# A last projection with 21 Strassen slabs in place of 17, and two of their block sums made by GpSimd's transfers

## The reference

```python
x = _layer_norm(DEEPNORM_ALPHA * x + mix, ln1_gain[l], ln1_bias[l])
h = jnp.square(jax.nn.relu(x @ w_ff1[l])) @ w_ff2[l]
x = _layer_norm(DEEPNORM_ALPHA * x + h, ln2_gain[l], ln2_bias[l])
```

## Time and profile before

| | us |
|---|---|
| median of 3 runs | 1241.91 (1241.68 to 1242.8) |
| the profiled execution | 1241.83 |
| its span, first to last instruction | 1240.0 |
| TensorE's granted clock | 0.999 of full speed |

### The profile page before, as it was taken

The page is one execution under the profiler, slowest core; times in us unless marked ns, Lnnn a source line. Parts: engine busy times, 40 slices in busy tenths (PEclk is TensorE's granted clock), DMA queues, the critical chain, the costliest instruction groups (busy, mean ns, idle before and its releaser), DMA issues.

```text
span 1240.0 us, 22985 instructions
## 1 busy us (share of the span) xinstructions
PE 1218.8 (98%) x9585; PEld 1031.9 (83%) x9585; DVE 861.9 (70%) x909; ACT 619.6 (50%) x674; POOL 137.5 (11%) x94
## 2 busy tenths in 40 slices
PE   8999999999999999999999999999999999999996
PEld 8888888888779778888888888888888888888884
DVE  5688887465766375765455555545689998899987
ACT  6754555545666254453434343343455555566651
POOL 0022112000000000055000000000122221022220
PEclk9999999999999999999999999999999999999999
DMA  9454465332421156635555555555565555555541
GB/s 339 150 210 170 172 252 189 104 138 104 170 103 54 54 215 234 242 110 196 192 180 201 174 200 177 195 186 186 199 245 203 202 203 204 188 208 200 200 155 68
DMA packets 34206, 222.38 MB, mean 179 GB/s; under 512 B 4717, under 2 KB 5101, under 8 KB 8782
## 3 DMA queue, kind: packets, MB, share of 16 engines
q1 hardware_dynamic: 34126, 221.21, 50.2%
HBM read 219.10 MB, written 2.10 MB: 178 GB/s over the span
## 4 chain that ended last, share of the span: by engine, by line
PE 55%; DVE 1%; ACT 0%; issue 0%; ACTq 0%; DVEq 0%
PE ps L531 55%; DVE stats L2139 0%; DVE xres L2136 0%; DVE wlo_end L2301 0%; DVE xres L2329 0%; DVE xres L2327 0%; ACT whi_end L1283 0%; DVE xres L2317 0%; ACT xres L1283 0%; DVE xres L2321 0%; ACT shi L1283 0%; DVE moments L2142 0%; PE ps L1175 0%; DVE moments L2149 0%; ACT moments L1283 0%
## 5 line engine op out<-in xcount | busy, mean ns | idle before, releaser
L1712 DVE TENSOR_TENSOR wlo<-stage,whi 128x2048 fp32r<-128x2048 f32 x166 | 387.2, 2333 | 245.7 <-ACT whi L1283 244.9
L531 PE MATMUL ps<-acts,whi 128*128 128x512 f32 (+1 forms) x1728 | 535.0, 392 | 3.4 <-DVE wlo L1739 2.1
L1283 ACT ACTIVATE whi<-stage 128x2048 fp32r<-128x2048 f32 (+2 forms) x196 | 361.9, 1848 | 308.7 <-PE ps L531 303.9
L531 PEld LDWEIGHTS ps<-acts,wlo 128*128 128x128 f32 x1680 | 315.8, 188 | 72.5
L531 PE MATMUL ps<-acts,wlo 128*128 128x256 f32 x1680 | 334.8, 278 | 0.0
L531 PEld LDWEIGHTS ps<-acts,whi 128*128 128x128 f32 x1728 | 264.0, 189 | 8.0 <-DVE wlo L1739 2.3
L531 PE MATMUL ps<-whi,shi 128*128 128x512 f32 x402 | 110.9, 389 | 0.6 <-issue 0.6
L531 PE MATMUL ps<-whi,slo 128*128 128x512 f32 x402 | 110.8, 389 | 0.0
L531 PE MATMUL ps<-wlo,shi 128*128 128x512 f32 x402 | 110.8, 389 | 0.0
L1283 ACT ACTIVATE shi<-hid 128x512 fp32r<-128x512 f32 x64 | 40.5, 632 | 124.1 <-PE ps L531 124.1
L531 PEld LDWEIGHTS ps<-whi,shi 128*128 128x128 f32 x402 | 75.3, 188 | 16.5 <-issue 1.0
(11 more groups left out here) (290 smaller groups left out, 1394.6 us busy)
## 6 DMA issues: line engine op xcount, KB each, us to landing
stage<-w_ff SPq DMA_DIRECT2D x128, 1024.0 KB, 4.8
stage<-w_in SPq DMA_DIRECT2D x48, 1024.0 KB, 4.9
stage<-w_out SPq DMA_DIRECT2D x16, 1024.0 KB, 4.9
stage<-w_in SPq DMA_DIRECT2D x6, 512.0 KB, 9.4
xstage<-xT SPq DMA_DIRECT2D x4, 512.0 KB, 7.4
TM_TT<-eyes SPq DMA_DIRECT2D x4, 512.0 KB, 7.7
xres<-x SPq DMA_DIRECT2D x1, 2048.0 KB, 9.6
gain<-ln_gain SPq DMA_DIRECT2D x2, 1024.0 KB, 7.3
```

The lines of the kernel that those rows point to most:

```text
L531: return pe.matmul(out, lhsT, rhs, start=start, stop=stop, skip_group_check=True)
L1283: return act.activation(out, in_, func, **kw)
L1712: TTn(wlo[k0 % NHL][:, :], stage[k0 % NST][:, :], f(whi[k0 % NHL][:, :]), ALU.subtract).then_inc(s_lo, 1)
```

## The change

The sets of Strassen slabs become 4, 6, 9, 11, ..., 26, 28 and 37, 39, ..., 57, 59: two of every five slabs. `tsum` gets a second buffer (in slot 9, part of the activations of the first projection; `bias2` lies there at the end). The two sums of L2250 go: POOL issues a transfer that copies two weight blocks from memory into `tsum`, and, when it has landed, one that adds a third block to both. Both wait for the landing of the one before. DVE waits for them on `s_lsum` and makes the other two sums. The order of ACT and DVE is changed where the last but one slab was a Strassen slab, for slabs 1 to 3 (pair before weights), and in the last turn (`whi_end`, `wlo_end` before the pair, the third part of `shared_taken` behind it). The loads of `gain2` and `bias2` move behind all slabs. Two semaphores of the start are merged.

```diff
--- before.py
+++ after.py
@@ -51,7 +51,7 @@
 G_END = G_FF2 + DFF // P
 NST, NHL = 4, 2
 
-QUADS = (tuple(range(4, 29, 3)), tuple(range(38, 60, 3)))
+QUADS = ((4, 6, 9, 11, 14, 16, 19, 21, 24, 26, 28), (37, 39, 42, 44, 47, 49, 52, 54, 57, 59))
 QUAD = QUADS[0] + QUADS[1]
 
 
@@ -213,7 +213,7 @@
         bias1 = at("bias1", 13, [P, D])
         shift_diag = at("shift_diag", 12, [P, P])
         shift_row = at("shift_row", 13, [P, 512])
-        tsum = at("tsum", 12, [P, 4, 512])
+        tsums = [at("tsum0", 12, [P, 4, 512]), at("tsum1", 9, [P, 4, 512])]
         thi, tlo = at("thi", 10, [P, 4, 512], F32R), at("tlo", 11, [P, 4, 512], F32R)
         asum = at("asum", 13, [P, 4, P], byte=2048)
         ashi = at("ashi", 13, [P, 4, P], F32R, byte=4096)
@@ -252,12 +252,12 @@
         s_x = [sem(f"x_loaded{i}") for i in range(4)]
         s_xhi, s_xlo = sem("head_piece_rounded"), sem("head_piece_remainder")
         s_cst, s_pos, s_attc, s_levc, s_gup = (
-            sem("consts_loaded"), sem("positions_loaded"), sem("attention_consts_loaded"),
+            sem("constants_and_lora_weights_loaded"), sem("positions_loaded"), sem("attention_consts_loaded"),
             sem("level_masks_loaded"), sem("gate_up_loaded"))
         s_ln1c, s_ln2c, s_xres, s_out = (
             sem("ln1_vectors_loaded"), sem("ln2_vectors_loaded"), sem("x_reloaded"), sem("output_stored"))
         s_vecl, s_lncol = sem("vectors_loaded"), sem("ln1_columns_loaded")
-        s_vec, s_lup = sem("zeros_then_vectors_ready"), sem("lora_weights_loaded")
+        s_vec, s_lsum = sem("zeros_then_vectors_ready"), sem("block_sums_loaded")
         s_lora, s_z, s_sig = sem("lora_activated"), sem("decay_logits"), sem("decay_sigmoid")
         s_item, s_itemd, s_gam = sem("rate_or_cumsum"), sem("rate_or_cumsum_done"), sem("chunk_decay_kept")
         s_ang, s_sin = sem("rotary_table_step"), sem("sines_ready")
@@ -463,8 +463,8 @@
             sp.dma_start(lncol[:, :, :], t["ln1_cols"]).then_inc(s_lncol, 16)
             slab_half(2, 0)
             slab_half(2, 1)
-            sp.dma_start(wup[:, :], t["w_up"]).then_inc(s_lup, 16)
-            sp.dma_start(aup[64:128, :], t["a_up"]).then_inc(s_lup, 16)
+            sp.dma_start(wup[:, :], t["w_up"]).then_inc(s_cst, 16)
+            sp.dma_start(aup[64:128, :], t["a_up"]).then_inc(s_cst, 16)
             sp.dma_start(cst[:, :], t["consts"][:, 0:C_SMALL]).then_inc(s_cst, 16)
             slab(3, 3, t["w_in"][3])
             sp.dma_start(posi[:, :], t["positions"].partition_broadcast(P)).then_inc(s_pos, 16)
@@ -514,11 +514,10 @@
             sp.dma_start(bias1[:, :], t["ln1_bias"].partition_broadcast(P)).then_inc(s_ln1c, 16)
             slabs(G_FF1, 1, N_FF1 // 2, t["w_ff1"])
 
-            slabs(G_FF2, 0, 2, t["w_ff2"])
-            sp.wait_ge(s_used, G_FF2)
+            slabs(G_FF2, 0, DFF // P // 4, t["w_ff2"])
+            sp.wait_ge(s_ql, 2 * len(QUAD))
             sp.dma_start(gain2[:, :], t["ln2_gain"].partition_broadcast(P)).then_inc(s_ln2c, 16)
             sp.dma_start(bias2[:, :], t["ln2_bias"].partition_broadcast(P)).then_inc(s_ln2c, 16)
-            slabs(G_FF2, 2, DFF // P // 4, t["w_ff2"])
             for i, (a, q) in enumerate(((0, 0), (0, 1), (0, 2), (0, 3), (1, 3), (1, 0), (1, 1), (1, 2))):
                 sp.wait_ge(s_lnd, i + 1)
                 sp.dma_start(t["out"][tok(a), quarter(q)], xres[:, a, quarter(q)]).then_inc(s_out, 16)
@@ -617,8 +616,7 @@
             first_chunk()
             second_chunk()
 
-            pe.wait_ge(s_cst, 16)
-            pe.wait_ge(s_lup, 32)
+            pe.wait_ge(s_cst, 48)
             pe.wait_ge(s_lora, 1)
             pe.wait_ge(s_vec, 2)
             for a in range(TT_):
@@ -1657,8 +1655,8 @@
                 k = quad_no(n)
                 if k:
                     act.wait_ge(s_used, G_FF2 + QUAD[k - 1] + 1)
-                act.wait_ge(s_qs, 3 * k + 3)
-                A(thi[:, :, :], tsum[:, :, :], ACT.Copy).then_inc(s_qh, 1)
+                act.wait_ge(s_qs, 2 * k + 2)
+                A(thi[:, :, :], tsums[k % 2][:, :, :], ACT.Copy).then_inc(s_qh, 1)
                 act.wait_ge(s_pl, 2 * NB + 3 * k + 3)
                 A(ashi[:, :, :], asum[:, :, :], ACT.Copy).then_inc(s_qh, 1)
 
@@ -1666,28 +1664,26 @@
 
                 act.wait_ge(s_used, G_FF2 + QUADS[h][-1] + 1)
                 act.wait_ge(s_ql, 2 * quads_to(h))
-                A(tsum[:, 0, :], ps[:, shared_bank(h, 0), :], ACT.Copy).then_inc(s_qh, 1)
+                A(tsums[0][:, 0, :], ps[:, shared_bank(h, 0), :], ACT.Copy).then_inc(s_qh, 1)
 
             for n in range(1, LAST_PAIR + 2):
                 g, m = G_FF2 + n, n % (DFF // P // 2)
-                if n == 4:
-                    act.wait_ge(s_ff, N_FF1)
+                if n <= 4:
+                    act.wait_ge(s_ff, n + 1 if n < 4 else N_FF1)
                 if n in QUAD:
                     split(hid[:, 2 * m:2 * m + 2, :], g, None, n % 2)
+                    if n - 2 in QUAD:
+                        quad_sums_hi(n)
                     hi_own(g)
                 elif n == LAST_PAIR + 1:
                     act.wait_ge(s_stage[g % NST], 16 * (g // NST + 1))
                     act.wait_ge(s_used, G_FF2 + QUAD[-1] + 1)
-                    split(hid[:, 2 * m:2 * m + 2, :], g, None, n % 2)
                     A(whi_end[:, :], stage[g % NST][:, :], ACT.Copy).then_inc(s_hi, 1)
-                elif n < 4:
-                    hi(g, g)
-                    act.wait_ge(s_ff, n + 1)
                     split(hid[:, 2 * m:2 * m + 2, :], g, None, n % 2)
                 else:
                     split(hid[:, 2 * m:2 * m + 2, :], g, None, n % 2)
                     hi(g, g)
-                if n + 1 in QUAD:
+                if n + 1 in QUAD and n - 1 not in QUAD:
                     quad_sums_hi(n + 1)
                 if n - 1 == QUADS[sweep(n)][-1]:
                     shared_copied(sweep(n))
@@ -2241,16 +2237,15 @@
 
                 g, k = G_FF2 + n, quad_no(n)
                 src = stage[g % NST][:, :].rearrange("p (j q) -> p j q", j=4)
+                tsum = tsums[k % 2]
                 if k == 0:
                     dve.wait_ge(s_ff, N_FF1)
-                    dve.wait_ge(s_lnp, 8)
-                else:
-                    dve.wait_ge(s_ql, 2 * k)
+                elif k > 1:
+                    dve.wait_ge(s_ql, 2 * k - 2)
                 dve.wait_ge(s_stage[g % NST], 16 * (g // NST + 1))
-                TTn(tsum[:, 0:2, :], src[:, 1::2, :], src[:, 0:1, :].broadcast_to([P, 2, 512]), ALU.add).then_inc(s_qs, 1)
-                dve.wait_ge(s_qs, 3 * k + 1)
+                dve.wait_ge(s_lsum, 32 * k + 32)
                 TTn(tsum[:, 2, :], tsum[:, 0, :], src[:, 3, :], ALU.add).then_inc(s_qs, 1)
-                dve.wait_ge(s_qs, 3 * k + 2)
+                dve.wait_ge(s_qs, 2 * k + 1)
                 TTn(tsum[:, 3, :], tsum[:, 2, :], src[:, 2, :], ALU.add).then_inc(s_qs, 1)
 
             def quad_sums_lo(n):
@@ -2259,14 +2254,14 @@
                 if k:
                     dve.wait_ge(s_used, G_FF2 + QUAD[k - 1] + 1)
                 dve.wait_ge(s_qh, rounded_count(n, 1))
-                TTn(tlo[:, :, :], tsum[:, :, :], f(thi[:, :, :]), ALU.subtract).then_inc(s_ql, 1)
+                TTn(tlo[:, :, :], tsums[k % 2][:, :, :], f(thi[:, :, :]), ALU.subtract).then_inc(s_ql, 1)
                 dve.wait_ge(s_qh, rounded_count(n, 2))
                 TTn(aslo[:, :, :], asum[:, :, :], f(ashi[:, :, :]), ALU.subtract).then_inc(s_ql, 1)
 
             def shared_taken(h, part):
 
                 top, right, bottom, corner = (xres[:, a, quarter(2 * h + q)] for a, q in ((0, 0), (0, 1), (1, 0), (1, 1)))
-                copied, v, z = (tsum[:, i, :] for i in range(3))
+                copied, v, z = (tsums[0][:, i, :] for i in range(3))
                 p1, p5, p7, p6 = (ps[:, shared_bank(h, i), :] for i in range(4))
                 if part == 0:
                     dve.wait_ge(s_ql, 2 * quads_to(h))
@@ -2290,22 +2285,24 @@
 
             for n in range(1, LAST_PAIR + 2):
                 g, after = G_FF2 + n, n - QUADS[sweep(n)][-1]
-                if n in QUAD:
+                if n in QUAD and n - 2 not in QUAD:
                     quad_sums_lo(n)
-                if n >= 4:
+                if n <= LAST_PAIR:
                     split(pair_of_hidden(n), n, n % 2, g - 1)
                 if n in QUAD:
+                    if n - 2 in QUAD:
+                        quad_sums_lo(n)
                     lo_own(g)
                 elif n == LAST_PAIR + 1:
                     dve.wait_ge(s_hi, g + 1)
                     TTn(wlo_end[:, :], stage[g % NST][:, :], f(whi_end[:, :]), ALU.subtract).then_inc(s_lo, 1)
+                    split(pair_of_hidden(n), n, n % 2, g - 1)
+                    shared_taken(1, 2)
                 else:
                     lo(g, g)
-                if n < 4:
-                    split(pair_of_hidden(n), n, n % 2, g - 1)
                 if n + 2 in QUAD:
```

(26 more changed lines are left out.)

## The result

The changed kernel is slower: 1277.71 us (median of 6 runs, 1271.88 to 1282.92) against 1243.15 us for the kernel before on the same chip (median of 6, 1241.68 to 1243.94), a ratio of 1.0278, 95% interval 1.0253 to 1.0303. The prediction was 1238.2 us in a range of 1235.9 to 1242.5. The profiled execution took 1277.78 us, with a span of 1275.9 against 1240.0.

What follows compares the result with a forecast made beforehand. PE, busy 98% of the span, was taken as the bound; -2.72 - 0.85 - 0.5 + 0.4 = -3.67 us against the profiled 1241.83, itself 0.08 below the median, gave 1238.2 us, range 1235.9 to 1242.5.

Steps and rivals of the forecast that it cites:

- C: Time per Strassen slab of POOL's serial chain of copy and adding transfer; put at 11.1 us, bounds 6.8 to 20.8.
- a chain over 13: Rival, chance 0.15: POOL's chain exceeds 13 us, DVE and then PE wait; at C = 14, +10.6 us, 1248.4.
- list of signs: Expected profile signs; PE waiting on DVE after slabs 11, 16, 21 or at 27 would show a late chain.
- POOL kept from issuing: Rival, chance 0.03: running DVE instructions delay each of POOL's two transfer issues; C = 15.7, +39.5 us, about 1277.
- Four more Strassen slabs: Last projection: 17 Strassen slabs become 21, each saving PE three matmuls; -2.72 us.
- Slab 1's hole: PE's 0.74 us wait ahead of slab 1 and slow start vanish as the hidden pair is split first; -0.85 us.
- End slabs: Last pair of slabs: reordering alone gains 2.4 us, but POOL's multiplies lengthen DVE's wlo and wlo_end; net -0.5 us.
- The clean tail: Rival, chance 0.16: POOL's multiplies miss DVE's row at the end or interfere less; -2.4 for -0.5, 1236.3 us.
- Slabs 26 to 28: Narrow place at slabs 24, 26, 28: DVE's work ends late; +0.4 us, and 2C - 22 more if C exceeds 11.
- The load queue and slab 37: Two loads leave SP's queue ahead of slab 8, and slab 37 replaces 38 as first; no cost, over 3 us room.
- The 0.75 us to spare at each second Strassen slab: At the second of two Strassen slabs around a plain one, DVE's steps need 5.6 us of 6.35; it fits.

Runs made afterwards that it cites:

- the two-buffer run: Changed kernel with its two buffers and a separate semaphore for adding transfers, so the next copy starts when its buffer is free; 1245.37 us, ratio 1.0012.
- POOL's multiplies last: Kernel with three buffers, POOL's two multiplies by gain2 held until DVE's last hidden remainder; 1239.26 us, ratio 0.9967.
- three buffers: Changed kernel with a third sums buffer, a separate semaphore for adding transfers, and copies issued two Strassen slabs ahead; 1241.48 us, ratio 0.9986.
- the old spacing: Changed kernel, transfers kept, with the 17 Strassen slabs of before (every third); 1243.18 us, ratio 0.9999.

## Why the prediction was wrong

**The step that failed is one price: the adding transfer.** I put "4.3 for the copy and 4.8, a 1 MB slab, for the adding one" and C = 11.1. With 1 us for its issue that was 5.8; it lands 8.8 us after the start of its issue, in the mean of the seven chains, with bytes half of the slab's. That is +3.0. The phase ahead of it, put at 5.3, took 5.99, +0.7: POOL's three sums lasted up to 4.5 us and not 3.5, with DVE's instructions beside them, and the copy up to 7.9. From each landing to the next copy's issue pass 0.57 us, for which I had nothing. Together 15.35. Of the 8.7 up to 1.8 is the adding itself (the plain copy's 6.9), and up to 1.9 the close spacing (6.8 at the old one); the two can overlap, and what the close spacing does to a transfer is not shown. My bounds, 6.8 to 20.8, held C; the value inside them was taken from rows of transfers that don't add, that SP issues, and that don't follow one of their own kind.

**The mechanism was right, as the rival "a chain over 13".** DVE at the wait, `slo` and `wlo` of the plain slab behind it, PE behind them, and a first pair (4, 6) that still has time in hand: all of it is in the trace, with the holes at slabs 10, 15, 20, just ahead of slabs 11, 16, 21, where the prediction's list of signs had them just behind. Its formulas, 8C - 108.8 for a sweep and C - 9.8 at slab 28, give 19.6 for the first sweep at 15.35 and 12.6 for the second at 15.18, 32.2 together; 22.0 and 12.6 were measured. So the rival's arithmetic was sound to 7%, though it knew nothing of the clock: 11.9 of the 34.6 are PE at half speed. My reading is that the two agree because the chain and not PE sets the pace: while POOL's transfers decide when a slab may begin, a slow stretch of PE eats waiting time that would have been there anyway. No run separates the clock from the waits. I gave this rival 0.15 and argued against it that the transfer would need 7 us, "1.5 times a slab of twice its bytes". It takes more.

**The number of the other rival is met by chance.** "POOL kept from issuing" said 1277 with C = 15.7. The number is luck twice over: C came near 15.7 by slow landings, and the early fall of the clock, which is no part of the change, made up 5 us of the 39.5. Its mechanism is not there: the issues take 749 to 904 and 1185 to 1218 ns in all 42, whatever DVE does beside them, and the two-buffer run has every issue still in place and none of the 33 us. The Trainium skill's "SBUF — State Buffer", section "Who interferes with whom", gives DVE's `tensor_tensor` no mode that would keep GpSimd from writing descriptors; the trace agrees, by the same 42 issues. The Trainium skill's page "DMA: Bandwidth & Descriptors", section "Anatomy of one DMA — SWDGE (gpsimd) path", would have given 3.2 us a transfer, an estimate; the copy took 4.7 and the adding one 8.7. So by that page the case looked safer than by my rows, and the measurement decides against both.

The other terms, one by one:
- Four more Strassen slabs, -2.72: right. With POOL's multiplies last, slab 4's `thi` matmul to slab 59's is 286.52 us for 288.31, that is -2.72 and the 0.92 lost at slab 28.
- Slab 1's hole, -0.85: measured -0.86.
- End slabs, -0.5: measured -0.56 up to the first row sum, with a hole of 1.66 us in the predicted 1.5 to 2. The cause is as predicted, POOL's multiplies on DVE's row, 1.1 us each, though they fell on two adds to the residual instead of `wlo` and `wlo_end`. They cost as much there, for DVE's row has no pause from 1240.3 us on, so that whatever is lengthened delays what PE waits for. The clean tail, -2.4, is to be had by one constant in a wait.
- Slabs 26 to 28, +0.4 at C = 11: 0.95 with the chain out of the way. DVE's sums were priced at 1.4 us; they take 1.8 (0.69 + 1.09 above) with POOL beside them.
- The load queue and slab 37: no wait of PE at either, as predicted.
- The 0.75 us to spare at each second Strassen slab: enough. With DVE relieved of 1.22 us and three buffers no pair but 26, 28 loses anything; with DVE making all the sums, two pairs of the first sweep overran by 0.55. The 0.75 itself is not measured.

What the prediction left out altogether is the clock: the holes of 2.29, 3.08, 3.49 and 5.26 us were each followed by a stretch at half speed, the one of 2.42 was not. So a wait of PE may cost more than its length where nothing else sets the pace, as behind the last shift's wait of 4.2 us, where the same six matmuls took 4.28 to 5.50 us.

## What to carry to other kernels

Before a pair of dependent transfers is put behind one counting semaphore, work out the period that the loop leaves for it, and price each transfer by one of its own kind, at the spacing that it will have (6.8 us became 8.7 here by the spacing alone). If no row has one, the risk lies in the ratio of period to price: in this kernel a chain of 14.0 us against a period of 12.92 cost 9.2 us, one of 15.35 cost 34.6. The cure cost one semaphore, and one more buffer for most of what was left, with the transfers as slow as ever: let the next copy start when its own buffer is free. And POOL's leftovers (here two multiplies) belong behind the last instruction of DVE that PE waits for.

## What the runs showed of the hardware

- A transfer issued by POOL that adds 512 KB into SBUF landed 6.1 to 13.1 us after the start of its issue: median 6.8 with 15.64 us for each chain, 8.7 serial and without a pause, 9.0 and 9.8 where the next copy could run beside it. A plain one of the same bytes in its place took 6.9 (5.1 to 8.7), and the copy ahead of it 4.1, 4.7 and 5.2 (3.9 to 8.2) in the old spacing, the changed kernel and the one with the plain second transfer. Half the bytes gave 6.5, in 128 pieces of 2 KB as in 256 of 1 KB.
- The price on POOL was 0.72 to 0.75 us for most plain issues (1.09 at most), 1.20 for the adding one, 0.90 for an adding one of 128 pieces.
- Two multiplies of 128 x 512 by POOL lengthened DVE instructions beside them by 0.8 to 1.1 us each (0.68 to 1.78, 2.29 to 3.38, 0.69 to 1.44).
- PE's granted clock fell for some microseconds early in the kernel (0.83 over 30 to 60 us) in two of the fourteen profiles and at 420 to 440 us (0.89) in a third. The two early falls follow the two longest waits of PE at that place (0.65 and 0.74 us, 0 to 0.59 in the others); that the wait sets the fall off is not shown. It shifted the start of slab 0 by 5 us, which is why spans are compared here from slab 0 on.
